# Nine matmuls of a second product moved behind the first step of the first one, and a row scale formed ahead of a table step

## What is computed

```python
h = _rms(x, g_mix[l])            # rows of x over their root mean square, times a gain
z = h @ w_in[l]                  # 1024 x 5120
za, zu, zv, zq, zg = jnp.split(z, SPLITS, axis=-1)
ya = jax.nn.gelu(_s5(za, ...))   # a diagonal state space model; its powers need cos/sin tables
yb = _sgu(zu, zv, ...)
yc = _mem_xattn(zq, mem, ...)
```

## Time and profile before

| what | value |
|---|---|
| device time, median of 3 runs | 769.4 us (769.1 to 769.69) |
| span of the profiled execution, first to last instruction | 768.0 us |
| TensorE busy | 759.7 us, 99% of the span |
| VectorE, ScalarE, GpSimd busy | 550.8, 355.4, 315.5 us |
| mean granted TensorE clock | 0.999 of full |

### The profile page before, as it was taken

The page is one execution under the profiler, slowest core; times in us unless marked ns, Lnnn a source line. Parts: engine busy times, 40 slices in busy tenths (PEclk is TensorE's granted clock), DMA queues, the critical chain, the costliest instruction groups (busy, mean ns, idle before and its releaser), DMA issues.

```text
span 768.0 us, 9764 instructions
## 1 busy us (share of the span) xinstructions
PE 759.7 (99%) x3562; PEld 629.0 (82%) x3562; DVE 550.8 (72%) x752; ACT 355.4 (46%) x529; POOL 315.5 (41%) x169
## 2 busy tenths in 40 slices
PE   8999999999999999999999999999999999999997
PEld 7788887788888888888888888888888888788886
DVE  6999997684848484246767777777777767746687
ACT  6896567644545433634343433332222323434554
POOL 4456655233333333444443444453545344840000
PEclk9999999999999999999999999999999999999999
DMA  8743333122222343232233886666656567768853
GB/s 271 298 150 130 117 96 114 33 88 82 83 83 76 123 143 99 83 101 91 83 110 110 273 297 223 231 206 203 213 180 211 179 204 237 283 193 252 296 202 126
DMA packets 42371, 126.17 MB, mean 164 GB/s; under 512 B 4192, under 2 KB 6368, under 8 KB 40544
## 3 DMA queue, kind: packets, MB, share of 16 engines
q1 hardware_dynamic: 42192, 125.45, 49.1%
q10 hardware_dynamic: 144, 0.26, 0.1%
HBM read 107.08 MB, written 18.61 MB: 164 GB/s over the span
## 4 chain that ended last, share of the span: by engine, by line
PE 89%; ACT 3%; DVE 3%; POOL 2%; DMA 1%; issue 1%; SPq 0%; ACTq 0%
PE bank L1633 24%; PE bank L1635 24%; PE bank L1634 24%; PE bank L1997 3%; PE bank L1999 3%; PE bank L1998 3%; ACT uc L649 1%; DVE s5p L1007 1%; POOL w_lo L579 1%; PE bank L1874 1%; PE bank L1749 1%; PE bank L1766 1%; DMA xT<-xt_dram 1%; ACT w_hi L589 1%; POOL lo_c L579 1%
## 5 line engine op out<-in xcount | busy, mean ns | idle before, releaser
L528 POOL TENSOR_TENSOR w_lo<-raw,w_hi 128x1024 fp32r<-128x1024 f32 x90 | 218.8, 2431 | 300.1 <-ACT w_hi L589 300.1
L589 ACT ACTIVATE w_hi<-raw 128x1024 fp32r<-128x1024 f32 x112 | 118.8, 1060 | 310.9 <-PE bank L1635 306.3
L1633 PE MATMUL bank<-h_hi,w_hi 128*128 128x512 f32 x608 | 238.5, 392 | 0.3 <-POOL w_lo L533 0.3
L1635 PE MATMUL bank<-h_hi,w_lo 128*128 128x512 f32 x608 | 236.6, 389 | 0.0
L1634 PE MATMUL bank<-h_lo,w_hi 128*128 128x512 f32 x608 | 236.6, 389 | 0.0
L1633 PEld LDWEIGHTS bank<-h_hi,w_hi 128*128 128x128 f32 x608 | 114.2, 188 | 24.6 <-issue 1.0
L1634 PEld LDWEIGHTS bank<-h_lo,w_hi 128*128 128x128 f32 x608 | 114.2, 188 | 23.8 <-issue 0.5
L1635 PEld LDWEIGHTS bank<-h_hi,w_lo 128*128 128x128 f32 x608 | 114.1, 188 | 23.6
L533 POOL TENSOR_TENSOR w_lo<-raw,w_hi 128x512 fp32r<-128x512 f32 x48 | 67.2, 1420 | 52.6 <-ACT w_hi L589 45.8
L1007 DVE TENSOR_TENSOR mix<-mix 128x512 f32<-128x512 f32 x44 | 44.9, 1020 | 13.3 <-DMA mix<-w_dram 12.1
L1007 DVE TENSOR_TENSOR lo<-raw,hi 128x1536 fp32r<-128x1536 f32 (+1 forms) x19 | 33.0, 1742 | 24.2 <-ACT hi L917 24.1
(11 more groups left out here) (319 smaller groups left out, 1398.0 us busy)
## 6 DMA issues: line engine op xcount, KB each, us to landing
raw<-w_dram SPq DMA_DIRECT2D x112, 512.0 KB, 3.4
mix<-w_dram SPq DMA_DIRECT2D x11, 1024.0 KB, 8.0
mix_dram<-mix SPq DMA_DIRECT2D x11, 1024.0 KB, 6.4
raw<-w_dram SPq DMA_DIRECT2D x30, 256.0 KB, 4.1
raw<-mix_dram SPq DMA_DIRECT2D x26, 256.0 KB, 4.0
half_dram<-odd SPq DMA_DIRECT2D x11, 256.0 KB, 8.2
second<-half_dram SPq DMA_DIRECT2D x3, 768.0 KB, 6.0
raw<-mix_dram SPq DMA_DIRECT2D x3, 768.0 KB, 4.3
```

The source lines that it names most:

```text
L528: nc.gpsimd.tensor_tensor(w_lo[:, s, :], raw[:, s, :], fv(w_hi[:, s, :]), ALU.subtract).then_inc(w_ready, 1)
L589: nc.scalar.activation(w_hi[:, slot, :], raw[:, slot, :], ACT.Copy).then_inc(w_rounded, 1)
L1633: mm(out, a[0], b[0], start=first, stop=False)
L1635: return mm(out, a[1], b[0], start=False, stop=last)
```

## The change

Half a tile of `zv`'s weights (the first 512 columns of tile 4) is loaded a second time, into a buffer of its own, `raw_v`, right behind the first k of x. ACT rounds it into `v_hi` after `h_hi` of k = 0, POOL makes `v_lo` after the first half of tile 0. The 9 matmuls that stood in `zv_step(0, range(3))` behind the eight steps of `za` stand behind the first of them, and read `v_hi` and `v_lo`. Tile 4 is still loaded, rounded and split whole, since the fourth token group reads it later. DVE does `x_scale` ahead of `table_step(1)` instead of inside `table_step(2)`, and `wide_rows` follows the last `za_step` directly. Some semaphores are merged into counting ones (`diag`, `wide_done`, `trig_ready`).

```diff
             for k in range(4):
                 load_first(k // 2, k % 2)
                 load_x(k)
+                if k == 0:
+                    sp.dma_start(raw_v[:, :], w_d[T_ZV, :, 0:WB]).then_inc(v_loaded, 16)
...
                     low_half(t, j).then_inc(done, 1)
+                    if t == 0 and j == 0:
+                        pool.wait_ge(v_rounded, 1)
+                        nc.gpsimd.tensor_tensor(v_lo[:, :], raw_v[:, :], fv(v_hi[:, :]), ALU.subtract
+                                                ).then_inc(v_ready, 1)
...
                 round_x(k)
+                if k == 0:
+                    act.wait_ge(v_loaded, 16)
+                    nc.scalar.activation(v_hi[:, :], raw_v[:, :], ACT.Copy).then_inc(v_rounded, 1)
...
-            def table_step(n, scale=None):
+            def table_step(n):
                 table_half(n, (0, 1))
                 go(table_sum(n, 0))
                 link(table_sum(n, 1))
-                if scale:
-                    scale()
                 turn_squared(ER, EI, ER, EI)
...
+            x_scale()
             table_step(1)
-            table_step(2, x_scale)
+            table_step(2)
             table_step(4)
-            dve.wait_ge(wide_x, 1)
+            dve.wait_ge(wide_done, 1)
...
-            for k in range(KD):
+            za_step(0)
+            x_hi, x_lo = h(0)
+            pe.wait_ge(v_rounded, 1)
+            for c in range(3):
+                mm(bank[4 + c][:, :], x_hi[:, c * P:(c + 1) * P], v_hi[:, :], start=True, stop=False)
+            for c in range(3):
+                mm(bank[4 + c][:, :], x_lo[:, c * P:(c + 1) * P], v_hi[:, :], start=False, stop=False)
+            pe.wait_ge(v_ready, 1)
+            for c in range(3):
+                mm(bank[4 + c][:, :], x_hi[:, c * P:(c + 1) * P], v_lo[:, :], start=False, stop=False)
+            for k in range(1, KD):
                 za_step(k)
...
-            pe.wait_ge(w_half, T_ZV + 1)
-            zv_step(0, range(3))
-            pe.wait_ge(diag_x, 1)
-            wide_rows(7, xdiag[:, :, :], T, wide_x)
+            pe.wait_ge(diag, 1)
+            wide_rows(7, xdiag[:, :, :], T, wide_done)
             tile_ready(T_ZV)
             zv_step(1, range(3))
             pe.wait_ge(rstd_ready, 1)
```

More of the change, by code:

```diff
@@ L212, in build @@
         std = at("std", o_s + (4 * C_BRE + 63) // 64 * 64, [P, T])
+        raw_v = at("raw_v", o_f + 2048, [P, WB])
+        v_hi = at("v_hi", o_f + 4096, [P, WB], R)
+        v_lo = at("v_lo", o_f + 6144, [P, WB], R)
         mstd = at("mstd", o_f, [P, M])
@@ L261, in build @@
         w_used = sem("w_used")
+        v_loaded, v_rounded, v_ready = sems("v_loaded v_rounded v_ready")
         X_PARTS = ((0, 1), (1, 2), (2, 3), (3, 4), (4, 6), (6, 8))
@@ L273, in build @@
         norms = {n: dict(zip(keys, sems(" ".join(f"{n}_{k}" for k in keys)))) for n, keys in NORM_KEYS.items()}
-        tok_sq, tok_std, diag_x, diag_m, wide_x, wide_m, rstd_ready, mrstd_ready = sems(
-            "tok_sq tok_std diag_x diag_m wide_x wide_m rstd_ready mrstd_ready")
+        tok_sq, tok_std, diag, wide_done, rstd_ready, mrstd_ready = sems(
+            "tok_sq tok_std diag wide_done rstd_ready mrstd_ready")
         za_taken, zv_taken, zq_taken, k_taken, v_taken, zu_scaled, zu_ready = sems(
@@ L282, in build @@
         pt_done, pt_act, pt_dve, pv_done, o_hi_s, o_lo_s = sems("pt_done pt_act pt_dve pv_done o_hi_s o_lo_s")
-        dt_ready, ang_ready, trig_ready = sems("dt_ready ang_ready trig_ready")
+        ang_ready, trig_ready = sems("ang_ready trig_ready")
         j1_g, j1_th, j1_merge = sems("j1_g j1_th j1_merge")
@@ L616, in _ @@
             act.wait_ge(vec_loaded, 16)
-            nc.scalar.activation(s5p[:, 0, :], small[:, C_LDT:C_LDT + 16], ACT.Exp).then_inc(dt_ready, 1)
+            nc.scalar.activation(s5p[:, 0, :], small[:, C_LDT:C_LDT + 16], ACT.Exp).then_inc(trig_ready, 1)
             for k in range(4):
@@ L1019, in _ @@
             dve.wait_ge(vec_loaded, 16)
-            dve.wait_ge(dt_ready, 1)
+            dve.wait_ge(trig_ready, 1)
             go(tt(XR, are, DT, ALU.mult))
@@ L1040, in _ @@
                 low_x(k)
-            dve.wait_ge(trig_ready, 1)
+            dve.wait_ge(trig_ready, 2)
             go(tt(ARE, MAG, CS, ALU.mult))
@@ L1121, in x_scale @@
             def x_scale():
-                token_scale(4, 1, tstd[:, :], trstd[:, :], xdiag[:, :, :], diag_x)
+                token_scale(4, 1, tstd[:, :], trstd[:, :], xdiag[:, :, :], diag)
+            x_scale()
             table_step(1)
-            table_step(2, x_scale)
+            table_step(2)
             table_step(4)
-            dve.wait_ge(wide_x, 1)
+            dve.wait_ge(wide_done, 1)
             V.tensor_copy(rstd[:, :], bank[7][:, :]).then_inc(rstd_ready, 1)
@@ L1136, in _ @@
                 low_tile(norms["m"], m_hi, m_lo, memf, C_GMEM, k)
-            token_scale(2, 2, mtstd[:, :], mtrstd[:, :], mdiag[:, :, :], diag_m)
+            token_scale(2, 2, mtstd[:, :], mtrstd[:, :], mdiag[:, :, :], diag)
             bre, bim, cre, cim = (grid(c0) for c0 in (C_BRE, C_BIM, C_CRE, C_CIM))
@@ L1165, in _ @@
             times([c[:, 0, :, :] for c in cpow], (cre, cim), ARE, AIM, True, 1)
-            dve.wait_ge(wide_m, 1)
+            dve.wait_ge(wide_done, 2)
             V.tensor_copy(mrstd[:, :], bank[3][:, 0:M]).then_inc(mrstd_ready, 1)
@@ L1721, in _ @@
                 if t == 3:
-                    pe.wait_ge(diag_m, 1)
+                    pe.wait_ge(diag, 2)
                     pe.wait_ge(za_taken, KB)
-                    wide_rows(3, mdiag[:, :, :], M, wide_m)
+                    wide_rows(3, mdiag[:, :, :], M, wide_done)
                 for j in range(2):
```

## The result

| what | before | changed |
|---|---|---|
| device time, median of 5 runs each | 769.4 us (769.1 to 769.71) | 776.18 us (775.73 to 777.07) |
| ratio, with its 95% interval | | 1.0087 (1.0076 to 1.0098) |
| span of the profiled execution | 768.0 us | 775.3 us (its time: 777.07) |
| mean granted TensorE clock | 0.999 | 0.994 |

The account below looks back on a forecast made before the run. TensorE, busy 99% of 768.0 us, was taken as the bound, its end hanging on `rstd`. 1.53 us gained and 2.1 lost gave +0.6; with 1.4 above the span and 0.1 more, 770.1 us, range 769.0 to 772.3.

Parts of the forecast that it names:

- the two closed holes: TensorE's idle 0.97 us before step 1 of `za` and 0.56 us before `wide_rows`; both forecast to close, gaining 1.53 us.
- tile 4's pair: POOL's two low halves of tile 4, forecast to still slow two DVE table operations, 2.15 us lost, once.
- The root's shift: ACT's root behind the four squares of `xtok`, forecast 0.63 us later, ending at 26.64; bounds 0.45 and 1.3.
- The later of the two decides, 0.63: Last `xtok` square: transfer 0.63 us later by 256 KB more in the queue, ACT's own path 0.45; the larger counts.
- the upper bound of 1.3: Largest root delay allowed, if `h_hi` of k = 1 is pushed back and step 1 starts at 11.9.
- A handover: From ACT's root to DVE's reciprocal: root ends at 26.64, reciprocal forecast to start at 26.69.
- Rival 1: POOL's tile 5 halves hold DVE's last table operations: 1.1 or 2.15 us on `rstd`, 771.2 to 772.3 us; chance 0.30.
- both shifts come from one queue: Argument against DVE meeting POOL's tile 5: POOL moves 0.63 us with the queue, DVE 0.59 with the root.
- Rival 3: TensorE's clock falls during its wait for `rstd`: 3 us of matmuls cost 1.5 us more, 771.6 us; chance 0.04.
- Hole C: TensorE's new wait for `rstd` after its early matmuls, from 33.08 to about 35.2, forecast at 2.1 us.
- the first of the two stretches: 764 to 766 us at the earlier span's end, without matmuls, granted clock 1.00; the next, 766 to 768, reads 0.70.
- the old stall: TensorE's wait released at 61.64 by ACT's rounding and POOL's low part; forecast to move to near 62.2.

Follow-up runs that it names:

- GpSimd kept out: The changed kernel with one more wait: GpSimd starts tile 5's two low halves only when `rstd` is ready; 772.5 us, ratio 1.0032.

## Why the prediction was wrong

**Right.** That the end of the span hangs on `rstd` and not on what TensorE saves: undoing the order leaves 770.05. TensorE's side up to `wide_rows` (30.29 against 30.08 forecast) and the two closed holes. That the added load, rounding and subtraction cost TensorE nothing in the first steps. That tile 4's pair still falls into the tables, once (1.28 and 1.35 us).

**The root's shift was mis-sized.** "The later of the two decides, 0.63" was 2.23, beyond the upper bound of 1.3. The last transfer was taken up 9.4 us after its issue at 16.1, where 7.9 after 15.3 had been read the earlier trace rows. The profiles of all kernels show how far the 256 KB explain it. In the eight that load them the root starts 0.48 to 2.23 us later than in the kernel before (25.71), 1.35 on average; in the four others that don't, from 0.31 sooner to 0.82 later, 0.24 on average. One execution of each was profiled. So the second load is worth about 1.1 us of the root by these means, an estimate and more than the 0.63, and the landing scatters by more than the whole term; that scatter was not in the range.

**A handover was taken as free.** "The root ends at 26.64, the reciprocal starts at 26.69": the rows have 0.09 there, not 0.05 (26.01 and 26.10), and that was read from an operation that did not wait for the root, only started near its end. Where VectorE stands waiting, the traces show 0.51 or 0.52, in the changed kernel and in six others.

**Rival 1 came in full.** It was priced rightly (2.15 forecast, 2.11 measured) and its condition was right: VectorE's shift more than 0.1 above GpSimd's. The shifts were 2.66 and 1.41 (tile 5's halves at 35.37 against 33.96). The step that failed is "against it, that by the rows both shifts come from one queue", with its chance of 0.30: VectorE moved with the root and the handover, GpSimd with the landing of tile 5, and the two moved by different amounts in each run, in the one with the order alone even in opposite directions (0.12 later, 0.57 sooner). The margin of 0.08 us between 33.88 and 33.96 is smaller than any of these. Taking GpSimd's pair away gave back exactly those 2.11 us. The Trainium skill, GPSIMD Engine Reference, section Specifications, has the shared interface, and the trace agrees; the rows add the size: a held operation of 0.2 us takes up to 1.3 us, and ends with GpSimd's instruction.

**Rival 3 came on top.** "Hole C of 2.1 us is about as long as the first of the two stretches": with 5 us it was not. The rivals were given one chance each, as if they excluded one another, but rival 1 lengthens the very hole on which rival 3 hangs. Its price was sized wrongly as well: 2.9 us, not 1.5. The sixteen starts from 39.40 to 45.80 take 6.40 us where the kernel before needs 3.50, so the clock stayed low for about 6 us; the 3 us of the forecast stood in no row. Nor did the comparison with the first stretch of the earlier trace rows bear the chance of 0.04: a hole of 2.81 us was enough in the kernel with GpSimd kept out.

**Not foreseen.** TensorE waits 0.80 us at 32.11 for the low half of tile 4, which followed the late root. It costs nothing here, because hole C lies behind it, but it would have been the next limit.

The sum by these terms, for the profiled execution: root 2.23, handover 0.43, collision 2.11, less 0.02 for the hole's edges (4.75 at TensorE), clock 2.9, less the old stall 0.41: 7.2 of 7.3 us. By the medians, the single line of order alone costs 4.5 us, the moved matmuls with the second load alone 0.3, both together 6.8. How the difference divides is open, and so are the scatter of the landing, why a hole of 3.07 us left the clock at 1.00 where one of 2.81 brought it down, and why executions of one kernel (order alone) differ by up to 3.1 us.

## What to carry to other kernels

An engine that fills a wait with unurgent work has margin; putting the waiting instruction first leaves the sum of the work equal and spends that margin, so each delay of what it waits for arrives in full. Where two engines miss each other by less than the terms of the sum, count the collision as happening. Let rivals add up where one creates the condition of the other: a longer TensorE hole costs its length and then the lower clock behind it. And postponing small work on an engine that is busy throughout moves the wait to a place that the early timeline doesn't show.

## What the hardware showed that was not expected

- A hole of 5 us in TensorE was followed by 14 matmuls at half rate, 0.427 us apart, and one of 2.81 us by 8. Behind holes of 2.71 and 3.07 us the profiled executions kept a clock of 1.00, while other executions of the same two kernels took 1 to 3 us longer. So in this range the length of the hole alone does not tell what the clock does.
- The warm-up matmuls at the start of the changed kernel took 0.21 us a record, the same form in the hole 0.12 (18 matmuls, 36 records in 4.18 us), though the granted clock reads 1.00 in both stretches. The column doesn't show the rate there:

```profile
1.10 4.17 PE L1711 MATMUL bank<-ones 128*128 128x128 f32 x20 [1.10 <-POOL eps L530]
```

```profile
2.00:6.00 4.00, 3.36 (x19) 3.17 (x18) 2.50 (x9) 1.86 (x5) 1.21 (x1) 1.00 0.90 274
```

- A VectorE instruction that waits for a ScalarE result (the reciprocal, for the root) starts 0.51 or 0.52 us after the end of the latter, in seven traces.
